# Softmax attentions: last head pair's projection split by head, its slabs spread over units 16 to 31, no filler matmuls

## The reference, cut to what matters

```
# differential attention (weights a_w_qkv, a_w_o): 8 heads, q and k 2 x 64 wide, v 128 wide
logits = einsum(q, k) + bias          # per block of 128 queries, causal
attn = softmax(logits[0]) - lam * softmax(logits[1])
o = rms_norm(attn @ v) * (1 - lambda_init);   out = o @ w_o
# forgetting attention (b_w_q, w_kvf, b_w_o): 16 heads, 64 wide
p = softmax(q @ k.T / 8 + c[t] - c[s]);       out = (p @ v) @ w_o
```

## Time and profile before

| | |
|---|---|
| median of 3 runs | 2497.06 us (2496.49 to 2499.13) |
| profiled execution | 2494.16 us |
| its span from first to last instruction | 2492.3 us |
| granted TensorE clock, mean | 0.996 |
| DVE, ACT busy | 54%, 30% |
| POOL busy | 65% |
| DMA queues q1 and q10 | 28.5% and 3.2% of 16 engines |

### The profile page before, as it was taken

How to read it: one execution, slowest core, us unless ns; L and a number is a source line. 1 busy time by engine, 2 the same in 40 slices (tenths; PEclk the granted TensorE clock), 3 DMA queues, 4 the chain that set the end, 5 groups by cost and what they waited for, 6 DMA issues and landing times.

```text
span 2492.3 us, 38543 instructions
## 1 busy us (share of the span) xinstructions
PE 2451.5 (98%) x13516; PEld 2001.4 (80%) x13516; DVE 1334.3 (54%) x1984; ACT 743.1 (30%) x1361; POOL 1615.4 (65%) x1548
## 2 busy tenths in 40 slices
PE   9999999999999999999999899999999999999998
PEld 7888888888778888887878688888877777888886
DVE  8777775535226333311555569884173345788812
ACT  3564552011232211101344434331032233343300
POOL 8756565755557777766544468887673435888864
PEclk9999999999999999999999999999999999999999
DMA  5433434332323333333322133333232222333321
GB/s 162 125 90 109 111 106 142 99 80 82 85 79 116 101 96 95 96 95 91 110 61 64 51 85 97 96 98 93 77 92 79 77 64 65 97 97 97 97 93 59
DMA packets 238100, 231.18 MB, mean 93 GB/s; under 512 B 16064, under 2 KB 230592, under 8 KB 237976
## 3 DMA queue, kind: packets, MB, share of 16 engines
q1 hardware_dynamic: 214528, 206.82, 28.5%
q10 hardware_dynamic: 23448, 22.61, 3.2%
HBM read 225.06 MB, written 4.84 MB: 92 GB/s over the span
## 4 chain that ended last, share of the span: by engine, by line
PE 70%; DVE 2%; ACT 1%; issue 0%; DMA 0%; SPq 0%; DVEq 0%; ACTq 0%
PE PS L672 42%; PE PS L663 5%; PE PS L664 5%; PE PS L667 5%; PE PS L656 4%; PE PS L747 3%; PE AUX L998 2%; PE AUX L1042 1%; PE AUX L1054 1%; PE AUX L1059 1%; DVE XT L1983 0%; PE AUX L775 0%; PE AUX L781 0%; PE AUX L1019 0%; PE AUX L1001 0%
## 5 line engine op out<-in xcount | busy, mean ns | idle before, releaser
L622 POOL TENSOR_TENSOR wlo<-raw,whi 128x512 fp32r<-128x512 f32 x772 | 1064.5, 1379 | 64.4
L620 POOL TENSOR_SCALAR whi<-raw 128x512 fp32r<-128x512 f32 x772 | 552.9, 716 | 785.7 <-issue 424.8
L672 PE MATMUL PS<-opA_hi,whi 128*128 128x512 f32 x1312 | 524.1, 400 | 1.1 <-DVE cu L1570 0.8
L672 PE MATMUL PS<-opA_hi,wlo 128*128 128x512 f32 x1312 | 511.8, 390 | 0.0
L672 PE MATMUL PS<-opA_lo,whi 128*128 128x512 f32 x1312 | 511.2, 390 | 0.0
L672 PEld LDWEIGHTS PS<-opA_hi,whi 128*128 128x128 f32 x1312 | 246.4, 188 | 60.2 <-issue 7.5
L672 PEld LDWEIGHTS PS<-opA_hi,wlo 128*128 128x128 f32 x1312 | 246.3, 188 | 52.7
L672 PEld LDWEIGHTS PS<-opA_lo,whi 128*128 128x128 f32 x1312 | 246.6, 188 | 49.6 <-issue 1.2
L2008 DVE SCALAR_TENSOR_TENSOR facc<-fu,vec,facc 128x512 f32<-128x512 f32 x176 | 217.3, 1293 | 15.6 <-ACT facc L1382 15.6
L663 PE MATMUL PS<-opA_hi,whi 128*128 128x512 f32 x560 | 221.1, 395 | 1.6 <-DVE XT L1875 0.8
L664 PE MATMUL PS<-opA_hi,wlo 128*128 128x512 f32 x560 | 218.3, 390 | 0.0
(11 more groups left out here) (321 smaller groups left out, 3762.4 us busy)
## 6 DMA issues: line engine op xcount, KB each, us to landing
raw<-in_w_in_dram SPq DMA_DIRECT2D x184, 256.0 KB, 2.8
raw<-in_ffn_w_in_dram SPq DMA_DIRECT2D x176, 256.0 KB, 2.8
raw<-in_ffn_w_out_dram SPq DMA_DIRECT2D x88, 256.0 KB, 2.6
raw<-in_a_w_qkv_dram SPq DMA_DIRECT2D x48, 256.0 KB, 2.7
raw<-in_w_ffn_gate_dram SPq DMA_DIRECT2D x44, 256.0 KB, 2.7
raw<-in_w_ffn_up_dram SPq DMA_DIRECT2D x44, 256.0 KB, 2.8
raw<-in_w_ffn_down_dram SPq DMA_DIRECT2D x44, 256.0 KB, 2.6
acs_row<-acs_dram ACTq DMA_DIRECT2D x16, 512.0 KB, 5.7
```

The costliest lines, as they stand in the source:

```text
L620: nc.gpsimd.tensor_scalar(whi[slot][:], raw[raw_slot][:], 1.0, 1.0, ALU.mult, ALU.mult).then_inc(w_high, 1)
L622: nc.gpsimd.tensor_tensor(wlo[slot][:], raw[raw_slot][:], whi[slot][:].bitcast(F32), ALU.subtract).then_inc(slab_split, 1)
L672: last = nc.tensor.matmul(psum_fm(key, panel, m), a, b[:, k, :], start=k + n == 0, stop=k == total - 1 and n == 2)
```

## The change

1. The query and key panels of the last pair (pair 3) are loaded and multiplied by head. Each half has two slabs of 4 chunks by 128 columns; a slab has the same bytes and the same 12 matmuls as before. The panels come in the order query of head 0, key of head 0, values, query of head 1, key of head 1.
2. In units 16 to 23 stands one slab each (head 0's two and two, then the four of the values). Units 24 and 25 hold two slabs each, those of head 1.
3. The evictions that fall due in units 23, 24 and 25 stand ahead of the next unit's M in the list, where the others stand behind D. Those of a half panel are one instruction instead of two.
4. The matmuls on constants in units 24 and 25 are gone.
5. The first two O and L move from units 24 to 26 into unit 26. The output slabs of units 27 to 30 stand ahead of V, where they stood behind it.

```diff
+K_HEAD = (2 * SLAB,) * (D // P // (2 * SLAB))
+def last_pair(names):
+    j = PAIRS - 1
+    q, k, v = names
+    return [((q, j, 0), 1, K_HEAD), ((k, j, 0), 1, K_HEAD), ((v, j), 1, K1024), ((q, j, 1), 1, K_HEAD), ((k, j, 1), 1, K_HEAD)]
...
@@ order2
-        fill = [("slab", (n, j + 1), 0, h) for n in names for h in range(4)] if j < PAIRS - 1 else []
+        if j < PAIRS - 2:
+            fill = [("slab", (n, j + 1), 0, h) for n in names for h in range(4)]
+        else:
+            fill = [t for k, _, c in last_pair(names)[:3] for h in range(len(c)) for t in (("slab", k, 0, h), None)]
...
-            fill = [None] * 2 + [("slab", project, n, k) for k in range(3) for n in range(2)]
+            fill = [("slab", k, 0, h) for k, _, c in last_pair(names)[3:] for h in range(len(c))]
+            out_slabs = [("slab", project, n, k) for k in range(3) for n in range(2)]
+            fill += [None, out_slabs[0]] + [t for x in out_slabs[1:5] for t in (x, None)] + [None, out_slabs[5]]
         for u in range(8 * j, 8 * j + 8):
+            if j == PAIRS - 1:
+                out += late
+                late = []
             if u < 31:
                 out.append(("M", u + 1))
...
+            if u == 26:
+                out += [("O", 0), ("O", 1)]
...
-            if u > 24:
-                out.append(("L", u - 25))
+            if u > 25:
+                out += [("L", 0)] * (u == 26) + [("L", u - 25)]
...
-                if fill and (j < PAIRS - 1 or part == "X"):
+                if fill:
...
-            if u in range(24, 31):
+            if u in range(26, 31):
                 out.append(("O", u - 24))
...
@@ scores
-                    if qb == 0 and hh == 0:
-                        pe.wait_ge(evicted, 2 * (max(PAN[(names[0], j)], PAN[(names[1], j)]) + 1))
+                    if qb == 0 and (hh == 0 or j == PAIRS - 1):
+                        pe.wait_ge(evicted, 2 * (max(PAN[ready_key(n, j, hh)] for n in names[:2]) + 1))
...
-                            if u in (24, 25):
-                                keep_warm(WARM_UNIT, 2)
...
@@ ACT, O
-                        act.wait_ge(slab_done, slab_end((names[2], PAIRS - 1), 0))
+                        act.wait_ge(slab_done, slab_end((names[1], PAIRS - 1, 1), 0))
...
@@ qkv2
-                name, j = key
+                name, j = key[:2]
...
-                for m in range(2):
-
+                for m in key[2:] or range(2):
+                    ps = psum_fm(key, 0, m if len(key) == 2 else 0)
```

More of the change, by code:

```diff
@@ L21 @@
 SLAB = 2
[L24 removed]
+WARM_FACTORS, WARM_RESIDUAL = 2, 12
 WARM_START = 6
@@ L277, in order2 @@
                     out.append(("X", done))
-                if fill and (j < PAIRS - 1 or part == "X"):
+                if fill:
                     t = fill.pop(0)
                     out += [t] * (t is not None)
-                    if t is not None and t[1] != project and t[3] == len(K1024) - 1:
+                    if t is not None and t[1] != project and t[3] == len(SPLIT[t[1]]) - 1:
                         late = [("epi", t[1], t[2])]
@@ L508, in source @@
             flat = (panel + 2 * i) * PANEL
+            head = key[2] * P if len(key) == 3 and a == PAIRS - 1 else 0
+            width = P if len(key) == 3 and a == PAIRS - 1 else PANEL
             twin = panel % 2, (panel // 2 + i) * PANEL
@@ L526, in source @@
             if name in ("q2", "k2", "v2"):
[L527 removed]
+                return W["a_w_qkv_2"], 0, ("q2", "k2", "v2").index(name) * D + a * PANEL + head, width
             if name in ("k3", "v3"):
[L529 removed]
+                return W["w_kvf_2"], 0, ("k3", "v3").index(name) * D + a * PANEL + head, width
             if name == "q3":
[L531 removed]
+                return W["b_w_q_2"], 0, a * PANEL + head, width
             if name == "f":
@@ L535, in source, with by_head @@
                       "fout": f"ffn_w_out_2_{a}"}[name]], 0, flat, PANEL
+        def by_head(slab):
+            return slab[:].rearrange("p c n -> p (c n)").rearrange("p (c n) -> p c n", n=P)
         def psum_fm(key, panel, m):
@@ L565, in fetch_slab @@
                 cols = slice(col, col + n) if isinstance(col, int) else bass.ds(col, n)
-                sp.dma_start(raw[s % RAW][:, 0:chunks, 0:n], w[:, c0:c0 + chunks, cols]).then_inc(w_loaded[s % RAW], 16)
+                slot = by_head(raw[s % RAW]) if n == P else raw[s % RAW][:, 0:chunks, 0:n]
+                sp.dma_start(slot, w[:, c0:c0 + chunks, cols]).then_inc(w_loaded[s % RAW], 16)
             def fetch(key, panel, i=0):
@@ L668, in chunk @@
                     return last
-                for m in range(1 if name in ("dt", "f") else 2):
+                one_head = SPLIT[key] == K_HEAD
+                if one_head:
+                    wh, wl = by_head(wh), by_head(wl)
+                for m in range(1 if name in ("dt", "f") or one_head else 2):
                     ah, al = wh[:, c, m * P:(m + 1) * P], wl[:, c, m * P:(m + 1) * P]
```

12 lines of the change are left out of this document (7 added, 5 removed).

## The result

The changed kernel takes 2500.18 us (median of 22 runs, 2496.07 to 2503.34), the kernel before 2496.71 us in runs beside it (22 runs, 2493.64 to 2499.13). The ratio is 1.0017, 95% interval 1.0011 to 1.0022: about 4 us slower, from 2.7 to 5.5. I had forecast 2496.8, no change. The measured time lies inside my range and inside the 0.2% that I had called no change, but with this many runs the slowdown is plain, and the forecast had the opposite sign. The profiled execution of after took 2500.1 us, with a span of 2498.3 and a mean granted clock of 0.995. The two profiled executions differ by 6.0 us where the medians differ by 3.5: that of before, 2494.16, is one of its faster runs, that of after lies at its median.

A forecast was written before the change was run, and what follows sets the result against it. PE, busy 98% of the span, was taken as the bound. First attention -2.5 and second +0.5 gave -2.0, or -0.3 with one fall: 2493.9 profiled, plus 2.9 gives a median of 2496.8 us, range 2492.8 to 2500.6.

The forecast's parts named there:

- The clock: Open term, both attentions: one half-clock fall counted, likelier in the first around units 24 to 26, at 1.7 us.
- one gap of 2.24 us, then work: Second attention, T of unit 26: its second half waits 2.24 us for W of unit 25, in place of 0.94.
- -0.8 with one fall: First attention's net: -0.8 us if the clock falls once again, -2.5 if it holds.
- all on PE's path: Constant matmuls of units 24 and 25: removing two groups per attention saves 3.02 us in the first, 3.04 in the second.
- the low part of the output operand: First O and L in unit 26: no cost expected; without PE's cover, one L of 0.6 us would show.
- +0.5: Second attention's net without a fall: 4.3 us closed, 4.8 us of new gaps; +2.2 with a fall.
- The step from profile to median: Whole kernel: the median of the runs was taken as 2.9 us above the profiled execution.
- The mechanism of an eviction ahead of M: Units 24 to 26: DVE's eviction waits for PE's last slab, delaying M and PE's next S; first-attention S gaps 1.43 to 1.67 us.
- The slower rival: Units 24 to 26, both attentions: clock falls after each eviction wait, six at 1.7 us, median 2505.3; chance 0.07.
- The faster rival: Both attentions: eviction waits do not show, gaining 11.4 us, median 2485.7; chance 0.11.
- The third rival: Both attentions: 6.1 us of constants only become gaps ahead of the same T and V, 2496.8 to 2497; chance 0.04.
- +1.4: Whole kernel: total change in us if both attentions fall to half clock, as the skill's rule would have it.

The follow-up runs named there:

- first-only kernel: The first attention as in the changed kernel, the second as in the kernel before: 2495.41 us, ratio 0.9998 to the kernel before.
- second-only kernel: The second attention as in the changed kernel, the first as in the kernel before: 2499.53 us, ratio 1.0013 to the kernel before.
- the last edit: 7 constant matmuls ahead of S of unit 1 of the second attention, added to the changed kernel with evictions behind M: 2485.06 us, ratio 0.9950 to before.

## Why the prediction was wrong

**The step that failed** is the one in "The clock": "I count one fall in the two attentions, likelier in the first", at 1.7 us. The first attention fell as I had it, for 3.4 us of half clock, at most 1.7 lost. In the second I had "one gap of 2.24 us, then work" (the X behind it has kept its 0.41 us from before, as I said) and gave it no fall in the likeliest case. It fell, and for 6.8 us, so the one fall cost 2.9. I had priced every fall by the only one that I had measured, 1.7 us in the earlier trace rows, and left the one at 1873.6, which I had seen, out of the count of two. Its length also changed between the profiles, from 3.4 to 6.8 us. The kernel with only the second attention changed shows both stretches again; one group of constants in unit 26 removes the later one; moving the key eviction removes it with its gap. That the first stretch of the second attention is the change's doing is not shown: it has 3.4 us in before and in the first-only kernel, 6.8 in after and the second-only kernel, none with constants back in units that lie far behind it. The later one is not the change's alone either: of the four profiles with the second attention's unit 26 as in before or without constants, one has 3.4 us there; of the three with the 2.37 us wait, all have it, for 3.4, 6.8 and 6.8 us. So the long wait goes with a likelier and longer fall, as far as seven profiles can tell.

**Terms of the sum that were off in size.** First attention: I had -0.8 with one fall in each kernel, and it is 0.0. The 3.02 us of constants were not "all on PE's path", as I had it: taken out alone they are worth nothing. They and the 0.77 at V of unit 24 could be counted only because a slab now fills that wait. The gaps that came sum to 0.78 + 1.44 + 1.59 + 1.84 + 1.54 + 0.34 + 0.78 = 8.31 us instead of 7.77. The largest part is the 0.34 us for the low part of the output operand, which I had costed at nothing because one L "would show" only if its cover were gone; then S of unit 28 with +0.17. The remaining 0.3 us has no gap of its own. Second attention: I had +0.5 and it is +1.7; S of unit 26 was 0.15 shorter, S of unit 27 and T of unit 26 0.07 and 0.13 longer, and gaps of 0.16 us ahead of two more T came. These make 0.4; another 0.8 has no gap of its own.

**The step from profile to median** was a term too: I added 2.9 us, as in before, and after's two figures are 0.1 apart.

**What was right.** The mechanism of an eviction ahead of M, with every place: S of units 26, 27 and 28 (1.43, 1.51 and 1.67 predicted; 1.44, 1.59 and 1.84 measured) and V of unit 26 (1.60; 1.54), and 1.13, 1.3 and 2.24 in the second (0.98, 1.37 and 2.37). No slab waited for a half panel. The page's 2.7 us is a median over 48 transfers of which eight are halves, so it does not show them; taken one by one, the 16 half slabs of both attentions landed in 2.7 to 3.0 us. One of them (the transfers issued from 1314 to 1317 us):

```profile
raw<-in_a_w_qkv_dram SPq DMA_DIRECT2D x1, 256.0 KB, 2.8
```

**The rivals.** The slower rival had the right direction, with six falls at 1.7. The profile has two in units 24 to 26, behind the third eviction of each attention, and none behind the other four; one of them is there in before too. The time is 2500.2 instead of 2505.3. The faster rival was wrong for this kernel, but its 11.4 us are about what the list gives when the evictions stand behind M. The third rival is refuted by the gaps at S, though the first attention's constants do turn into a gap where nothing else is changed. The rule of the Trainium skill, page "TensorE: Matmul & The Clock Gate", Part 1, is that the throttled state is the default and activity releases it; it spoke against the change. By it I had +1.4, with the right sign. That both attentions fell agrees with it, but before had a fall in the first too, with the constants left in; and before without its constants had 10.2 us of half clock in the first attention, yet none in unit 26 of the second.

**How much of the median is clock** stays open between about 1 and 3 of the 3.5 us. In the profiled executions it is 4.3 of 6.0. The mean granted clock of the runs, known to three places for each, averages 0.9945 over the 22 runs of after and 0.9950 over the 75 runs of before that stand beside the experiments. That is 13.6 and 12.5 us lost, 1.1 more. It may hide more: clock lost behind the second attention costs next to nothing (that part takes 420.3 us in before with 5.6 us lost, 420.0 in after with 3.4), and if after loses 2.2 less there in every run, the rest of it loses 3.3 more. The runs of either kernel scatter by 5.5 to 7.3 us, and stretches of half clock come and go elsewhere as well: ahead of the first attention the profiles lost from 0 to 5.1 us. Gaps and constants account for 1.7 us in the profiles, which would leave 1.8 for the clock; that lies between, and the runs settle it no further.

## What to carry to other kernels

In an in-order queue, put an eviction that waits for TensorE's latest work behind the step that frees TensorE's next product: here that alone turned +4 us into some -9. Price a wait on TensorE by its length and, as a second term with a chance of its own, by a stretch of half clock; take that stretch's length and how often it comes from several profiles, not from one (here none, 3.4 or 6.8 us in the same place). Compare gaps and clock in separate columns, since two profiles of one stage can differ by 3 us of clock alone. And before carrying a difference of two profiles over to the medians, see where each profiled run lies among its own.

## What was not expected of the hardware

- Half clock came in stretches of 3.4, 6.8 and once 10.2 us in the two attentions. At the start of the second, which only the last edit touches, it lasted 3.4 us in eight of the 13 profiles, 6.8 in three and was absent in two.
- A stretch of 3.4 us came behind gaps of no more than 0.93 and 0.41 us (the kernel before with more constants in the first attention), and none behind gaps of 1.44 and 1.59 us (with the key eviction moved).
- Where another engine's chain sets the pace it costs little: 10.2 us of it left the stage at 194.32 us. Where TensorE works through, it cost somewhat less than half its length: 1.4, 1.5 and 1.6 us for 3.4 us more of it (stages of 195.88, 194.48, 193.01, 199.78 and 198.22 us), 2.8 or 2.9 for 6.8.
- Constant matmuls laid into a wait of the second attention were followed by full clock in the three kernels that had them there (windows of 1.00 above), and by half clock in the first when 2.10 us of waiting remained behind them.
- Transfers whose rows are 512 bytes landed in 2.7 to 3.0 us, about as those with 1 KB (2.7).
